# Attention in a two-layer block: scores of the two components in one paired group or one after the other with a turn between

## The chip, the cores and the metric

The kernel runs on one core of a Trainium2 chip. The metric is the device time of one execution in microseconds; lower is better. A whole block of two layers is one launch. The change touches one stage of it, the attention of the first layer.

## What is computed

The reference adds 16 meta tokens to 1024 tokens of width 1024 and runs two layers. The first mixes by a state space model (S5) and, beside it, by differential attention; the second by a gated recurrence; behind each mixer stand a projection, a norm, a router and a mixture of experts. All of it is in float32. The attention has 4 heads; a head has two components of 64 dimensions each for queries and keys, and one set of values of 128 dimensions:

```python
def block(args):
    q_blk, c_blk = args
    s = jnp.einsum('bqhcd,bkhcd->bchqk', q_blk, k) * scale
    mask = cid[None, :] <= c_blk[:, None]
    p = jax.nn.softmax(jnp.where(mask, s, NEG_INF), axis=-1)
    w = p[:, 0] - lam * p[:, 1]
    return jnp.einsum('bhqk,bkhe->bqhe', w, v)
```

Two softmaxes are taken over the same keys, one for each component, and their difference with a learned factor weighs the values. The mask lets a query see its own chunk of 64 tokens and all chunks before it.

## The kernel before

The stages run one behind the other, with a barrier between them. `attention` (line 633) is cut into 36 units, a unit being a head and a tile of queries. Tile 0 has the 16 meta tokens, tiles 1 to 8 have 128 queries each. A unit with tile `qi` needs the first n = 16 + 128 qi keys, so n runs through 16, 144, 272, ..., 1040. Heads 0 to 2 take their tiles in rising order, head 3 in falling order (line 660).

For a unit u the work passes over three engines:

- TensorE, `scores(u)` (line 700): for each component c a matmul of the queries (64 rows of the array: rows 0 to 63 for c = 0, rows 64 to 127 for c = 1) with up to 512 keys at a time, into the PSUM area `S[(2u + c) % 3]` of 1024 columns. There are three such areas. A second, short matmul of `hide` and `ones` (48 or 64 columns, for n = 528 another of 16) adds the mask to the last chunk. For n = 1040 the last 16 keys go into a small area of their own, `tail`. The matmuls of the two components are written in turns: one of c = 0, one of c = 1, for the same part of the keys, the last part first. A float32 matmul has two records in the trace, a transpose has one.
- VectorE, `minimum(u, c)` (line 851): the row minimum of a component's scores (scores are kept with their sign turned by the scale -1 of the exponential).
- ScalarE, `exps(u, c)` (line 799): the exponential of the scores from PSUM into `prob`, with the row sums. Its end (`exp_done`) gives the area of PSUM free.
- VectorE, `combine(u)` (line 870): the two components into one tile of weights `w`.
- TensorE, `turn(u, j)` (line 729): transposes of up to four blocks of `w` into the one PSUM area `tp`; ScalarE and VectorE in turns copy it away (`copies`, line 775). A unit with more than four blocks has two or three such groups j.
- TensorE, `weigh(u, j)` (line 742): turned weights times values, into `po`; ScalarE's `out` (line 812) takes the result away, VectorE's `square` (line 886) sums its squares.

Each engine runs its own list in order, and semaphores tie them together. On TensorE the list (lines 757 to 764) is: scores of unit u + 1, then by groups the turn of unit u - 1 and the products of unit u - 2. `scores(u)` waits once, for `exp_done` of 2u - 1: the exponential of component 0 of the unit ahead, which frees the area of its own component 1.

```python
for u in range(-1, U + LAG):
    if u + 1 < U:
        scores(u + 1)
    for j in range(max(groups)):
        if 0 <= u - LAG + 1 < U and j < groups[u - LAG + 1]:
            turn(u - LAG + 1, j)
        if 0 <= u - LAG < U and j < groups[u - LAG]:
            weigh(u - LAG, j)
```

Of the kernel before, what the change touches and what calls it, by code (L numbers as in the profile page):

```python
# [632 lines left out]
def attention(nc, K, A):  # L633
# [12 lines left out]
    hide, ones = at("hide", [P]), at("ones64", [64])  # L646
# [13 lines left out]
    units = [(hd, qi) for hd in range(HEADS - 1) for qi in range(NT)] + [(HEADS - 1, qi) for qi in reversed(range(NT))]  # L660
    U = len(units)
    groups = [-(-(qi + 1) // PER) for _, qi in units]
    first_group = [sum(groups[:u]) for u in range(U + 1)]
    tails = [sum(qi == NT - 1 for _, qi in units[:u]) for u in range(U + 1)]
    with ExitStack() as ctx:
        S = [ctx.enter_context(nc.psum_tensor(f"scores{i}", [P, WIDE], F32)) for i in range(3)]
# [5 lines left out]
        @block.sync  # L672
        def _(sp):
            with nc.allow_non_contiguous_dma(reason="small parameters"):
                for i, n in enumerate(("lq1", "lk1", "lq2", "lk2")):
                    sp.dma_start(lq[i][:], A["l0_da_" + n].rearrange("(a d) -> a d", a=1).to_broadcast([P, HEAD_DIM])).then_inc(loaded, 16)
                sp.dma_start(g[:], A["l0_da_subln_g"].rearrange("(p a) -> p a", a=1)).then_inc(loaded, 16)
            load_w_out(sp, K, 0)
# [11 lines left out]
        def cuts(u):  # L690
            q0, m = TILES[units[u][1]]
            n = q0 + m
            ends = list(range(0, n, 512)) + [n]
            return q0, m, n, list(zip(ends, ends[1:]))

        @block.tensor
        def _(pe):
            pe.wait_ge(hide_made, 4)

            def scores(u):  # L700

                hd, qi = units[u]
                q0, m, n, parts = cuts(u)
                if u:
                    pe.wait_ge(exp_done, 2 * u - 1)
                if n > WIDE and u > LAG + 1:
                    pe.wait_ge(o_copied, u - LAG - 1)
                rows = [slice(64 * c, 64 * c + 64) for c in range(2)]
                if n > WIDE:
                    for c in range(2):  # L710
                        pe.matmul(tail[0:m, c, :], K.qT[rows[c], hd, q0:q0 + m], K.kT[rows[c], hd, WIDE:n], start=True, stop=False)
                        pe.matmul(tail[0:m, c, :], hide[rows[c], 0:m], ones[rows[c], 0:n - WIDE], start=False, stop=True).then_inc(tail_made, 1)
                        pe.wait_ge(tail_made, 2 * tails[u] + c + 1)
                for a, b in reversed(parts):
                    if a >= WIDE:
                        continue
                    place = lambda c, a, b: S[(2 * u + c) % 3][0:m, a:b]
                    lo = max(a, n - 64) if qi else b
                    for c in range(2):
                        last = pe.matmul(place(c, a, b), K.qT[rows[c], hd, q0:q0 + m], K.kT[rows[c], hd, a:b], start=True, stop=lo >= b)  # L720
                        if lo >= b and a == 0:
                            last.then_inc(s_ready, 1)
                    if lo < b:
                        for c in range(2):
                            last = pe.matmul(place(c, lo, b), hide[rows[c], 0:m], ones[rows[c], 0:b - lo], start=False, stop=True)
                            if a == 0:
                                last.then_inc(s_ready, 1)

            def turn(u, j):
                hd, qi = units[u]  # L730
                q0, m = TILES[qi]
                n = first_group[u] + j
                if j == 0:
                    pe.wait_ge(w_ready, u + 1)
                if n:
                    pe.wait_ge((turned_a, turned_v)[(n - 1) % 2], (n - 1) // 2 + 1)
                for kt in range(PER * j, min(PER * j + PER, qi + 1)):
                    k0, kk = TILES[kt]
                    last = pe.transpose(tp[0:kk, kt % PER, 0:m], w[u % 2][0:m, k0:k0 + kk], K.ident[0:m, 0:m])
                last.then_inc(turned, 1)  # L740

            def weigh(u, j):
                hd, qi = units[u]
                m = TILES[qi][1]
                n = first_group[u] + j
                pe.wait_ge((turned_a, turned_v)[n % 2], n // 2 + 1)
                if j == 0 and u:
                    pe.wait_ge(o_copied, u)
                if j == 0 and tails[min(u + LAG + 2, U)]:
                    pe.wait_ge(tail_done, tails[min(u + LAG + 2, U)])  # L750
                for kt in range(PER * j, min(PER * j + PER, qi + 1)):
                    kk = TILES[kt][1]
                    last = pe.matmul(po[0:m, :], wT[u % 2][0:kk, kt, 0:m], K.v_rows[0:kk, kt, P * hd:P * hd + P], start=kt == 0, stop=kt == qi)
                if j == groups[u] - 1:
                    last.then_inc(o_ready, 1)

            for u in range(-1, U + LAG):
                if u + 1 < U:
                    scores(u + 1)
                for j in range(max(groups)):  # L760
                    if 0 <= u - LAG + 1 < U and j < groups[u - LAG + 1]:
                        turn(u - LAG + 1, j)
                    if 0 <= u - LAG < U and j < groups[u - LAG]:
                        weigh(u - LAG, j)

            for i in range(NT):
                q0, m = TILES[i]
                pe.wait_ge(on_ready, i + 1)
                if i >= 2:
                    pe.wait_ge(oT_copied, i - 1)  # L770
                for h in range(HEADS):
                    last = pe.transpose(S[i % 2][:, P * h:P * h + m], o_sb[0:m, i, P * h:P * h + P], K.ident[0:m, 0:m])
                last.then_inc(oT_ready, 1)
# [1576 lines left out]
```

## Time and profile before

| what | value |
|---|---|
| median of 3 runs | 2592.74 us (2589.94 to 2603.44) |
| the profiled execution's own time | 2592.88 us |
| its span | 2591.1 us |
| mean granted clock of TensorE over the span | 0.937 |
| TensorE busy over the span | 2293.0 us, 88% |
| attention, from its first matmul to its last product | 352 to 557 us |

A granted clock of 1 is 2.4 GHz, one of 0.5 is 1.2 GHz. In the trace's views "idle before" stands in brackets behind a row, with the operation that ended the idle time; x4 is a count of records merged into one row, whose time runs from the first start to the last end. A form such as 64*128 64x512 is an array tile of 64 rows and 128 columns, through which 512 columns stream. Ends of matmuls are modelled; the distance between starts tells how long the array streamed.

### The profile page before, as it was taken

How to read it: one execution, taken by the hardware profiler on the slowest of the kernel's cores; microseconds unless marked ns; L12 is line 12 of the kernel's file. 1: busy time of each engine (PE TensorE's matmuls, PEld its weight loads, DVE VectorE, ACT ScalarE, POOL GpSimd, SP SyncE). 2: the span in 40 equal slices, each digit the busy share in tenths (PEclk: the TensorE clock that was granted, in tenths of full speed). 3: DMA queues.
4: the chain of work that ended last, by engine and by line, in shares of the span. 5: the costliest groups of instructions: out<-in, count | busy, mean ns of one | idle time of the engine just before them, and what ended most of it. 6: DMA issues, size and time to landing. Idle time of an engine off the chain costs nothing. (4 is left out here: it accounts for less than half of the span.)

```text
span 2591.1 us, 33356 instructions
## 1 busy us (share of the span) xinstructions
PE 2293.0 (88%) x13399; PEld 1284.7 (50%) x13399; DVE 819.2 (32%) x1629; ACT 488.7 (19%) x894; POOL 307.9 (12%) x265
## 2 busy tenths in 40 slices
PE   6999977889958999999968999999976999999984
PEld 4788535554545445445524555554444445545441
DVE  5652135543251111111107455554333101111115
ACT  2222123331101000000003444441110000000001
POOL 5252000001101101110002000001100111111102
PEclk9999988899968999999988999999977999999997
DMA  4100010011239998998948211111209998999965
GB/s 144 35 33 1 17 67 1 1 29 42 73 139 390 421 405 346 410 409 363 412 188 260 66 35 28 29 38 47 65 17 385 420 412 340 411 410 369 412 270 211
DMA packets 141990, 528.01 MB, mean 204 GB/s; under 512 B 38098, under 2 KB 61170, under 8 KB 125456
## 3 DMA queue, kind: packets, MB, share of 16 engines
q1 hardware_dynamic: 115632, 465.57, 45.9%
q0 software_dynamic: 13600, 40.52, 4.1%
q10 hardware_dynamic: 12608, 19.82, 2.3%
q8 instruction: 107, 1.75, 0.3%
q14 instruction: 43, 0.35, 0.0%
HBM read 492.04 MB, written 40.50 MB: 206 GB/s over the span
## 5 line engine op out<-in xcount | busy, mean ns | idle before, releaser
L1698 PE MATMUL l_main_pgu<-l_w_ring,l_ex_xT 128*64 128x256 f32 (+1 forms) x4992 | 489.2, 385 | 15.7 <-DMA l_w_ring<-in_l_moe_w_gate 13.5
L1698 PEld LDWEIGHTS l_main_pgu<-l_w_ring,l_ex_xT 128*64 128x64 f32 (+1 forms) x4992 | 294.2, 130 | 200.8 <-issue 40.7
L1744 PE MATMUL l_main_py<-l_w_ring,l_ex_hT 128*64 128x512 f32 (+1 forms) x1248 | 239.3, 595 | 1.6 <-DVE l_ex_hT L1803 1.6
L1695 PE MATMUL l_main_pgu<-l_w_ring,l_ex_xT 128*128 128x512 f32 x384 | 177.6, 618 | 20.8 <-DMA l_w_ring<-in_l_moe_w_gate 20.8
L1803 DVE COPY l_ex_hT<-l_main_ph 128x256 f32<-128x256 f32 (+1 forms) x78 | 36.3, 466 | 419.8 <-PE l_main_ph L1719 419.8
L1799 DVE TENSOR_TENSOR l_ex_hid<-l_ex_sil,l_main_pgu 128x256 f32<-128x256 f32 (+1 forms) x78 | 36.1, 462 | 351.6 <-PE l_main_pgu L1698 270.2
L2130 PE MATMUL lru_pr<-h2T,lru_wz 128*128 128x352 f32 (+1 forms) x480 | 143.2, 459 | 3.8 <-ACTq L2179 3.8
L1744 PEld LDWEIGHTS l_main_py<-l_w_ring,l_ex_hT 128*64 128x64 f32 (+1 forms) x1248 | 71.5, 128 | 136.6 <-issue 129.6
L2135 PE MATMUL lru_pg<-h2T,lru_wz 128*128 128x512 f32 x320 | 139.0, 592 | 0.0
L1695 PEld LDWEIGHTS l_main_pgu<-l_w_ring,l_ex_xT 128*128 128x128 f32 x384 | 74.2, 198 | 113.4 <-issue 88.0
L1780 ACT ACTIVATE l_ex_sil<-l_main_pgu 128x256 f32<-128x256 f32 (+1 forms) x78 | 32.5, 417 | 486.3 <-PE l_main_pgu L1698 336.6
L1643 POOL DMA_INDIRECT expert_rows<-l_ex_yb,half_row x66 | 66.1, 1002 | 444.0 <-issue 219.6
L2130 PEld LDWEIGHTS lru_pr<-h2T,lru_wz 128*128 128x128 f32 x480 | 91.6, 192 | 53.8 <-ACTq L2179 4.2
L2009 PE MATMUL l_cps<-l_y,ident 128*128 128x512 f32 (+1 forms) x136 | 68.5, 659 | 53.3 <-DMA l_y<-expert_rows 53.3
L283 PE MATMUL s_pa<-hT,w_in 128*128 128x260 f32 x512 | 114.7, 383 | 0.0
L985 POOL TENSOR_TENSOR H<-H,l_ln_bias 128x1024 f32<-128x1024 f32 (+1 forms) x30 | 70.6, 2353 | 352.4 <-DVE H L973 352.4
L1050 PE MATMUL lru_pr<-w_out,y1T 128*128 128x512 f32 x240 | 106.5, 601 | 0.0
L283 PEld LDWEIGHTS s_pa<-hT,w_in 128*128 128x128 f32 x512 | 96.9, 190 | 16.4 <-issue 1.7
L2135 PEld LDWEIGHTS lru_pg<-h2T,lru_wz 128*128 128x128 f32 x320 | 60.8, 190 | 73.6 <-issue 71.8
L1630 POOL DMA_INDIRECT l_ex_xb<-h_rows,x_idx x38 | 37.4, 984 | 412.6 <-PE l_main_px L1667 262.5
L1766 ACT COPY l_ex_xT<-l_main_px 128x512 f32<-128x512 f32 (+1 forms) x52 | 27.5, 529 | 285.4 <-PE l_main_px L1667 285.4
L720 PE MATMUL scores<-kT,qT 64*128 64x512 f32 (+5 forms) x224 | 59.6, 615 | 17.6 <-ACT prob L807 14.7
(420 smaller groups left out, 2821.1 us busy)
## 6 DMA issues: line engine op xcount, KB each, us to landing
l_w_ring<-in_l_moe_w_gate SPq DMA_DIRECT2D x64, 2048.0 KB, 19.1
l_w_ring<-in_l_moe_w_up SPq DMA_DIRECT2D x64, 2048.0 KB, 23.5
l_w_ring<-in_l_moe_w_down SPq DMA_DIRECT2D x64, 2048.0 KB, 21.2
l_y<-expert_rows ACTq DMA_DIRECT2D x32, 512.0 KB, 6.5
h_rows<-H SPq DMA_DIRECT2D x24, 512.0 KB, 5.2
lru_wz<-in_l_w_in SPq DMA_DIRECT2D x20, 512.0 KB
w_in<-in_l_w_in SPq DMA_DIRECT2D x3, 2048.0 KB, 8.4
w_out<-in_l_w_out SPq DMA_DIRECT2D x2, 2560.0 KB, 12.6
```

The costliest lines, as they stand in the source:

```text
L283: last = pe.matmul(pa[n % 2][:, 0:STEPS], w[:, k, P * (f % HEADS):P * (f % HEADS) + P], hT[:, k, j, :], start=k == 0, stop=k == KD - 1)
L720: last = pe.matmul(place(c, a, b), K.qT[rows[c], hd, q0:q0 + m], K.kT[rows[c], hd, a:b], start=True, stop=lo >= b)
L985: pool.tensor_tensor(z, z, self.bias[0:m, :], ALU.add).then_inc(self.h_ready, 1)
L1050: last = pe.matmul(po[j % 2][h][0:m, :], self.slices[k][:, t0:t0 + m], self.w_out[:, k, 512 * h:512 * h + 512], start=k == 0, stop=k == ns ...
L1630: pool.indirect_dma_start(xb[xn % 2][0:m, :], None, K.h1_dram, bass.IndirectOffsetOnAxis(ap=index, axis=0)).then_inc(gathered[xn % 2], 16)
L1643: pool.indirect_dma_start(y_halves, bass.IndirectOffsetOnAxis(ap=K.half_row[:, it.column:it.column + 1], axis=0), yb[i % 2][:, 0:512], Non ...
L1695: last = pe.matmul(out[:], x[:, k, :], w[0][:, k, :], start=k == 0, stop=k == KD - 1)
L1698: last = pe.matmul(out[HALF * h + o:HALF * h + o + m, 0:256], x[:, k, it.at + o:it.at + o + m], w[n][:, k, 256 * h:256 * h + 256], start=k ...
L1744: last = pe.matmul(py[b][HALF * h + o:HALF * h + o + m, :], hT[:, c % 2, HALF * (c // 2) + o:HALF * (c // 2) + o + m], ws[n][:, c, 512 * h ...
L2009: last = pe.matmul(ps[i % 2][h][0:m, :], K.ident[0:m, 0:m], y[j % YB][0:m, 512 * h:512 * h + 512], start=k == 0, stop=k == 1)
L2130: last = pe.matmul(pr[j][:, 0:c], wz[par][:, k, 0, :], K.hT[:, k, o:o + c], start=k == 0, stop=k == KD - 1)
L2135: last = pe.matmul(pgt[j][:, 0:c], wz[par][:, k, 1, :], K.hT[:, k, N_META + o:N_META + o + c], start=k == 0, stop=k == KD - 1)
```

## The change

On TensorE alone, `scores(u)` becomes three pieces. `score_tail(u)` holds the matmuls for the last 16 keys of the largest tile, with their wait. `scores(u, c)` holds all parts of one component, the first keys first, and waits for `exp_done` of x - 2 with x = 2u + c, which is what frees area x % 3. For c = 1 this is the wait of before; for c = 0 it is one exponential earlier. The semaphore `s_ready` still counts one for each component, in the same order. In the list of the engine, component 0 of unit u + 1 comes first, then the first turn of unit u - 1, then component 1 of unit u + 1, then the first products of unit u - 2. The other engines' code is the same.

```diff
--- before.py
+++ after.py
@@ -697,12 +697,10 @@
         def _(pe):
             pe.wait_ge(hide_made, 4)
 
-            def scores(u):
+            def score_tail(u):
 
                 hd, qi = units[u]
                 q0, m, n, parts = cuts(u)
-                if u:
-                    pe.wait_ge(exp_done, 2 * u - 1)
                 if n > WIDE and u > LAG + 1:
                     pe.wait_ge(o_copied, u - LAG - 1)
                 rows = [slice(64 * c, 64 * c + 64) for c in range(2)]
@@ -711,20 +709,23 @@
                         pe.matmul(tail[0:m, c, :], K.qT[rows[c], hd, q0:q0 + m], K.kT[rows[c], hd, WIDE:n], start=True, stop=False)
                         pe.matmul(tail[0:m, c, :], hide[rows[c], 0:m], ones[rows[c], 0:n - WIDE], start=False, stop=True).then_inc(tail_made, 1)
                         pe.wait_ge(tail_made, 2 * tails[u] + c + 1)
-                for a, b in reversed(parts):
+
+            def scores(u, c):
+
+                hd, qi = units[u]
+                q0, m, n, parts = cuts(u)
+                x, rows = 2 * u + c, slice(64 * c, 64 * c + 64)
+                if x >= 3:
+                    pe.wait_ge(exp_done, x - 2)
+                area = S[x % 3]
+                for a, b in parts:
                     if a >= WIDE:
                         continue
-                    place = lambda c, a, b: S[(2 * u + c) % 3][0:m, a:b]
                     lo = max(a, n - 64) if qi else b
-                    for c in range(2):
-                        last = pe.matmul(place(c, a, b), K.qT[rows[c], hd, q0:q0 + m], K.kT[rows[c], hd, a:b], start=True, stop=lo >= b)
-                        if lo >= b and a == 0:
-                            last.then_inc(s_ready, 1)
+                    last = pe.matmul(area[0:m, a:b], K.qT[rows, hd, q0:q0 + m], K.kT[rows, hd, a:b], start=True, stop=lo >= b)
                     if lo < b:
-                        for c in range(2):
-                            last = pe.matmul(place(c, lo, b), hide[rows[c], 0:m], ones[rows[c], 0:b - lo], start=False, stop=True)
-                            if a == 0:
-                                last.then_inc(s_ready, 1)
+                        last = pe.matmul(area[0:m, lo:b], hide[rows, 0:m], ones[rows, 0:b - lo], start=False, stop=True)
+                last.then_inc(s_ready, 1)
 
             def turn(u, j):
                 hd, qi = units[u]
@@ -756,10 +757,13 @@
 
             for u in range(-1, U + LAG):
                 if u + 1 < U:
-                    scores(u + 1)
+                    score_tail(u + 1)
+                    scores(u + 1, 0)
                 for j in range(max(groups)):
                     if 0 <= u - LAG + 1 < U and j < groups[u - LAG + 1]:
                         turn(u - LAG + 1, j)
+                    if j == 0 and u + 1 < U:
+                        scores(u + 1, 1)
                     if 0 <= u - LAG < U and j < groups[u - LAG]:
                         weigh(u - LAG, j)
```

What moves on TensorE, at a large tile: first head, n = 912 (scores in parts of 512 and 400), with the turn of the tile of 656 keys and the products of the one of 528. Before:

```order
L720 MATMUL scores<-kT,qT 128x400 x2
L725 MATMUL scores<-ones_2689,hide 128x64 x2
L720 MATMUL scores<-kT,qT 128x512 x2
L739 MATMUL turned_w<-ident,w_rows_2678 16x128
L739 MATMUL turned_w<-ident,w_rows_2678 128x128 x3
L753 MATMUL weighed<-v_rows,w_cols_2679 128x128 x4
L739 MATMUL turned_w<-ident,w_rows_2678 128x128 x2
L753 MATMUL weighed<-v_rows,w_cols_2679 128x128
```

With the change:

```order
L725 MATMUL scores<-kT,qT 128x512
L725 MATMUL scores<-kT,qT 128x400
L727 MATMUL scores<-ones_2689,hide 128x64
L740 MATMUL turned_w<-ident,w_rows_2678 16x128
L740 MATMUL turned_w<-ident,w_rows_2678 128x128 x3
L725 MATMUL scores<-kT,qT 128x512
L725 MATMUL scores<-kT,qT 128x400
L727 MATMUL scores<-ones_2689,hide 128x64
L754 MATMUL weighed<-v_rows,w_cols_2679 128x128 x4
L740 MATMUL turned_w<-ident,w_rows_2678 128x128 x2
L754 MATMUL weighed<-v_rows,w_cols_2679 128x128
```

The rows with x2 were one matmul of each component next to each other. Now all of component 0 stands ahead of the turn (`turned_w`) and all of component 1 behind it, ahead of the first products (`weighed`).

At a small tile, second head, n = 272, where the turn in front is that of the 16 meta tokens and the products are those of the largest tile (nine blocks in three groups). Before:

```order
L720 MATMUL scores<-kT,qT 128x272 x2
L725 MATMUL scores<-ones_2689,hide 128x64 x2
L739 MATMUL turned_w<-ident,w_rows_2678 16x16
L753 MATMUL weighed<-v_rows,w_cols_2679 128x128 x9
```

With the change:

```order
L725 MATMUL scores<-kT,qT 128x272
L727 MATMUL scores<-ones_2689,hide 128x64
L740 MATMUL turned_w<-ident,w_rows_2678 16x16
L725 MATMUL scores<-kT,qT 128x272
L727 MATMUL scores<-ones_2689,hide 128x64
L754 MATMUL weighed<-v_rows,w_cols_2679 128x128 x9
```

The second component's two matmuls moved behind the turn; nothing else did.

## Rows read from the trace of the kernel before

**Rows 1.** The page, busy us (share of the span) and instructions of an engine.
```profile
PE 2293.0 (88%) x13399; PEld 1284.7 (50%) x13399; DVE 819.2 (32%) x1629; ACT 488.7 (19%) x894; POOL 307.9 (12%) x265
```

**Rows 2.** Busy time by stretch, attention: length, busy us and instructions, clock, DMA.
```profile
352.00:558.00 206.00, 157.89 (x940) 108.37 (x940) 112.91 (x327) 84.03 (x249) 0.14 (x1) 0.83 0.06 22
```

**Rows 3.** Waits in 352 to 558 us: who waited for whom, us, times, longest.
```profile
ACT prob L807 <- DVE row_min L859: 52.6, 52, 3.2
...
PE scores L720 <- ACT prob L807: 14.7, 11, 8.9
...
PE turned_w L739 <- ACT w_cols L792: 11.7, 10, 2.1
PE turned_w L739 <- DVE w_cols L792: 10.9, 6, 3.6
```

**Rows 4.** TensorE in time, one tile of head 1: start, us, what [idle before].
```profile
418.36 0.52 PE L720 MATMUL scores<-kT,qT 64*128 64x144 f32 x4 [0.42 <-ACT prob L807]
...
418.87 1.08 PE L720 MATMUL scores<-kT,qT 64*128 64x512 f32 x4
419.88 0.60 PE L739 MATMUL turned_w<-ident,w_rows 128*16 128x128 f32 x4
...
421.87 0.73 PE L720 MATMUL scores<-kT,qT 64*128 64x272 f32 x4 [0.33 <-ACT prob L807]
```

**Rows 5.** TensorE in time, the projection behind attention.
```profile
568.74 3.59 PE L1050 MATMUL l_po<-w_out,yT 128*16 128x512 f32 x8 [1.57 <-PEq L2275]
572.17 3.60 PE L1050 MATMUL l_po<-w_out,daT 128*16 128x512 f32 x8
```

**Rows 6.** TensorE's busy time by stretch, cut at starts of units.
```profile
361.40:374.60 13.20, 10.77 (x54) 0.54 0.59 216
374.60:382.80 8.20, 7.02 (x47) 1.00 0.00 0
382.80:400.70 17.90, 13.79 (x68) 0.81 0.01 1
400.70:421.90 21.20, 18.50 (x146) 1.00 0.00 1
421.90:451.90 30.00, 20.57 (x92) 0.72 0.00 1
451.90:480.00 28.10, 25.31 (x169) 0.88 0.00 1
480.00:528.30 48.30, 35.94 (x188) 0.81 0.00 1
528.30:553.00 24.70, 23.30 (x170) 0.95 0.01 2
```

**Rows 7.** The nine stretches at half clock, first and last, and their sum.
```profile
352.00:373.00 21.00, 9.51 (x50) 0.53 0.57 207
...
526.50:529.90 3.40, 3.40 (x23) 0.60 0.02 5
sum 72.20, PE 51.58; mean PE 5.73
```

**Rows 8.** TensorE in time, large tiles of head 1.
```profile
427.54 0.33 PE L739 MATMUL turned_w<-ident,w_rows 128*128 128x128 f32 x1 [2.05 <-DVE w_cols L792]
427.80 1.37 PE L720 MATMUL scores<-kT,qT 64*128 64x400 f32 x4
...
429.28 2.03 PE L720 MATMUL scores<-kT,qT 64*128 64x512 f32 x4
...
435.56 0.69 PE L739 MATMUL turned_w<-ident,w_rows 128*128 128x128 f32 x2 [2.28 <-DVE w_cols L792]
...
440.22 2.08 PE L720 MATMUL scores<-kT,qT 64*128 64x512 f32 x4
```

**Rows 9.** The projection: its stretch, and a group of its records with its shape.
```profile
568.70:582.50 13.80, 13.76 (x32) 1.00 0.63 132
...
L1050 PE MATMUL l_po<-w_out,yT 128*16 128x512 f32 x16 | 7.2, 592 | 1.6 <-PEq L2275 1.6
```

## Prediction

> **What bounds the kernel now.** I read the page first. TensorE is busy for 88% of the whole span [rows 1], but this change touches one stage, so that share says nothing about it. The busy time by stretch comes next. Attention lies at 352 to 558 us, 206 us in which the array is busy for 157.9, VectorE for 112.9, ScalarE for 84.0, at a mean granted clock of 0.83 [rows 2]. No engine is full: the stage is a ring of waits. The view of waits names them [rows 3]: ScalarE's exponentials wait for VectorE's minima (52.6 us), the scores for the exponentials (14.7, of which 8.9 is the single wait in the opening, for small parameters), and the turns for the copies that ScalarE and VectorE make of the turn ahead (11.7 and 10.9). The order of the array's work in time shows where: between small tiles it waits 0.4 us or nothing, between large ones 2 us and more [rows 4, 8].
>
> The same view shows what the two components do. At full clock four records of 64x512 (two matmuls, one of each component, in two passes each) begin at 418.87 and the next work begins at 419.88: 1.0 us for four [rows 4]. One record of 512 columns alone takes 0.43 (eight from 568.74 to 572.17, all begun within 3.43 us [rows 5]), so four in a row would take 1.7. The two components, one in the upper 64 rows of the array and one in the lower, now stream side by side.
>
> The last thing to see is the clock. It is 1.2 GHz (granted 0.5) in an opening stretch, 352 to 373, and in eight later ones; all nine are 72.2 us with 51.58 of busy array, so the eight are 51.2 us with 42.1 of busy array [rows 7]. Ahead of them stand waits: 2.05 us ahead of 427.54, where a pair of 512 then takes 2.03 us rather than 1.1, and 2.28 ahead of 435.56 [rows 8].
>
> **Part 1, the pair is taken apart: cost.** No matmul is added; the count of passes is the same. But a component's passes now stream alone. With 0.43 us for 512 columns and two passes for a matmul, a component of n columns adds 4n/2400 us of array time at full clock, and its masking matmul (48 to 64 columns) some 0.11. Over 36 units n adds up to 18,944 (at most 1024 counts, since the tail's 16 columns were never paired): 31.6 us, and 3.4 for 32 masks, 35 in all, twice that at half clock. Idle array time takes part of it up. By stretches cut at starts of units [rows 6], idle is the length less the busy time:
> 361.4 to 374.6, n = 144 to 528, at half clock: adds 5.3, idle 2.4, leaves 2.9.
> 374.6 to 382.8, n = 656 and 784: adds 2.6, idle 1.2, leaves 1.4.
> 382.8 to 400.7, n = 912 and 1040: adds 3.4, idle 4.1, leaves 0.
> 400.7 to 421.9, n = 16 to 656: adds 3.9, idle 2.7, leaves 1.2.
> 421.9 to 451.9, n = 784 to 1040: adds 4.9, idle 9.4, leaves 0.
> 451.9 to 480.0, n = 16 to 784: adds 5.3, idle 2.8, leaves 2.5.
> 480.0 to 528.3, five large units: adds 8.3, idle 12.4, leaves 0.
> 528.3 to 553.0, n = 656 to 144: adds 3.9, idle 1.4, leaves 2.5.
> That is **10.5 us** later. If none could be hidden it would be 35 and more; if all, 0.
>
> **Part 2, the turn between the components.** The array goes from scores to turn to scores to products: two more changes a unit between matmuls that use 64 rows and ones that use all. The trace has the price of one: the lone turn at 427.54 has 128 columns, 0.11 us of streaming, and the scores behind it begin at 427.80, so 0.15 goes for the change [rows 8]. The other kind, from scores to full height, is bounded by 0 and the same 0.15; I take 0.05, since the turn at 419.88 begins as soon as two pair steps of about 0.5 have streamed [rows 4]. 0.2 in each of the 24 units of the stretches that have no idle left is **4.8 us**; in the large units it is covered.
> The Trainium skill speaks against this placing: "TensorEngine Tiling (Array Packing)", section Key Properties, says that a change of tiling mode, and not just of tile, drains the array. An estimate by it: the drain is what a record lasts (0.59 us by the mean of its group [rows 9]) beyond the 0.43 to the next start, 0.16, twice a unit, 24 times: 7.7 us in place of 4.8, and the forecast would be 3 us later.
> By queue: the second component's scores now stand behind the turn, which waits until its weights are combined and the previous turn is copied away. VectorE takes the minimum of the second component only after the first one's and after the combining of the tile ahead (lines 895 to 901), so a turn of 0.6 us in front of those scores [rows 4] should delay nobody while the array runs at full clock. I cost it at nothing; where that cover is thin, it shows as a wait for the second component's scores. No DMA and no other queue is touched.
>
> **Part 3, the head start.** The first component now waits only for its own area, one exponential earlier than before, and is ready when its own passes are (0.43 a step, where a pair takes 0.5 [rows 4, 5]). In the 12 units with n of 784 and more VectorE gets it about 0.2 us sooner for that: **-2 us**. Bounds: 0, and the 5.8 us of waits for exponentials that stand outside the opening [rows 3].
>
> **Part 4, the clock: the term that decides.** The waits that stand ahead of the slow stretches are the idle time which the added passes fill: 1.3 to 1.7 us of them a unit at n = 784 to 1040, against waits of 2.05 and 2.28 [rows 8]. If the later slow stretches go, 42.1 us of busy array at half clock becomes 21: up to **-21 us**. The lower end is 0, or worse, as a rival. The opening stretch follows the wait for parameters and stays. Whether a pass that fills half the array keeps the clock up is not shown in this stage, where it never runs alone for long. The nearest row is the projection behind the stage: 32 records of 128*16, an eighth of the array's columns, fill 568.7 to 582.5 and the clock stays 1.00 [rows 5, 9]. A partly filled array counted as active there, so I take it that it does here.
> The Trainium skill, "TensorE: Matmul & The Clock Gate", Part 1, has the throttled state as the default and activity as what lifts it; it does not say how half the rows count.
>
> **Sum.** 10.5 + 4.8 - 2 - 21 = -7.7; the profiled execution took 2592.88 us (1.8 outside its span) and the median of the three shown is 2592.74, so they stand together. 2592.9 - 7.7 = 2585.2; I round the head start up a little, since its bound is far, and forecast **2584.5 us**. A measurement of this kernel can tell about 0.5%, 13 us, from no change.
>
> **Rivals.**
> A, the clock does not follow, slower. If a pass of 64 rows alone counts for half of what a full one does, a unit's activity is what it was, the stretches stay, and the time runs longer with the added passes in them. Then 10.5 + 4.8 - 2, and 3 more for the units in slow stretches, where the addition (3.4 us for n = 1024) outgrows the idle time of some: +16, **2609 us**. For it: nothing in the stage shows a lone half-height pass; against: rows 5 and 9. The point from which it decides: if less than 13 of the 21 us come back, the kernel is slower than before. Partly so (half the stretches go) is +3, 2596. Chance of this rival 0.2.
> B, the large units shorten too, faster. There the ring of minimum, exponential, copy and turn sets the pace, and the first component may start one exponential earlier. If each of the 12 units with n of 784 and more gains 0.6 us beyond the forecast, it is -7 more: **2577 us**. For it: minima and copies are the largest waits of the stage [rows 3]; against: the turn behind the first component still waits on what it waited on. Chance 0.2.
> C, the passes were never free side by side: if the pair shares one stream, a lone pass of 512 takes 0.25 and not 0.43, nothing is added, and it is -23, **2570 us**. Against: a pair's 1.0 us is just over two lone full-height steps (0.86), which is what two streams of their own give; for a shared one, half-height passes would have to stream at twice the rate of rows 5. Chance 0.03.
>
> **How the numbers follow.** Forecast 0.57, A 0.2, B 0.2, C 0.03. The forecast's own range is -16 to +3 (the clock's term between two thirds and all, the covered part up or down by 5). 8 in 10 are held by 2573 to 2608: from just below B to A. Faster by over 0.5% (below 2579.8): C, over half of B and a quarter of the forecast, 0.28. Slower by over 0.5% (above 2605.7): most of A, 0.14. The same: 0.58.
>
> **What would show it.** In the changed profile: the scores' records of the two components apart, each record of 512 columns 0.43 after the last; array busy in the stage some 15 us above 157.9 even with a higher clock; mean granted clock of the stage 0.92 or more, with only the opening low; small units longer (n = 656: 3.5 us from 418.36 to 421.87 now, 4.3 then), large ones shorter (the 12.4 us of n = 912 from 427.80 to 440.22 becomes 9 or less) [rows 4, 8]. If the clock's mean stays at 0.83, Part 4 is wrong; if small units keep their length, Part 1 is.

## The result, and the profile after

| | before | with the change |
|---|---|---|
| median | 2591.94 us (4 runs) | 2646.28 us (2642.2 to 2665.33, 4 runs) |
| ratio, 95% interval | | 1.0206 [1.0165, 1.0247] |
| profiled span | 2591.1 us | 2646.8 us |
| attention: first score matmul to first projection matmul | 216.5 us | 263.9 us |
| the same stretch, time at 1.2 GHz | 78.5 us | 160.4 us |
| span behind it | 2022.4 us | 2030.1 us |

The kernel is some 54 us slower. The stage that the change touches is 47.4 us longer in the profiled executions. The 8 us behind it are in stages whose code is the same; in the twelve experiments below that part lies between 2016 and 2027 us, so the 2030 of this execution is just above all of them. I put it down to the difference between executions; no run shows its cause.

The page's row for TensorE, against [rows 1]:

```profile
PE 2378.4 (90%) x13399; PEld 1340.9 (51%) x13399; DVE 821.2 (31%) x1629; ACT 489.5 (18%) x894; POOL 307.8 (12%) x265
```

The stage by stretch (length, busy us and instructions of TensorE, weight loads, VectorE, ScalarE, GpSimd, then clock and DMA), to be read beside [rows 2]:

```profile
352.00:616.00 264.00, 243.87 (x976) 166.93 (x976) 121.59 (x338) 91.42 (x259) 0.57 (x4) 0.70 0.05 17
```

VectorE and ScalarE did nearly what they did before (118.8 and 90.1 us over the same instructions in the kernel before, 352 to 568.7), while TensorE is busy for 243.9 us of 264: it is now the bound. Its mean granted clock in the stage is 0.70.

The stage cut where the granted clock changes, TensorE alone; this answers to [rows 6, 7] (left out are 489.6 to 496.4, with a slow stretch of 3.4 us from 493, and what follows 602.2, with one of 10.2):

```profile
353.00:421.30 68.30, 59.48 (x162) 0.51 0.18 64
421.30:438.40 17.10, 17.10 (x111) 0.97 0.00 0
438.40:489.60 51.20, 49.72 (x132) 0.51 0.00 1
496.40:530.50 34.10, 33.10 (x178) 0.99 0.00 1
530.50:557.80 27.30, 26.73 (x72) 0.52 0.00 1
557.80:602.20 44.40, 43.08 (x256) 0.99 0.00 1
```

In the slow stretches the array is all but full: 49.72 us of 51.2 in the one from 438.4. Before the change, slow stretches followed waits and lasted 3.4 to 10.2 us, with the opening one of 20.5 the longest. Now one lasts 51 us with next to no wait in it, and the opening one 68, with one long wait, the 8.2 us for small parameters.

At three of the four rises of the clock (421.3, 489.6, 557.8) TensorE had just run turns and products of the full height one after the other, with no scores between them. Ahead of 489.6:

```profile
485.59 2.37 PE L754 MATMUL weighed<-v_rows,w_cols 16*128 16x128 f32 x8
488.02 0.90 PE L740 MATMUL turned_w<-ident,w_rows 128*128 128x128 f32 x3
488.72 1.06 PE L754 MATMUL weighed<-v_rows,w_cols 128*128 128x128 f32 x4
```

(The first row carries the form of its first record; the products behind it use 128 rows.) Where it falls at 438.4, there is no wait in the 17.1 us ahead; the last 4.1 of them hold scores of 64 rows, two transposes and one product of 16 rows.

TensorE in time, at a large tile at half clock (395.54 on, n = 912) and at a small one at full clock (434.27 on, n = 400), against [rows 4, 8]:

```profile
395.54 3.41 PE L725 MATMUL scores<-kT,qT 64*128 64x512 f32 x4
398.75 0.53 PE L727 MATMUL scores<-ones,hide 64*128 64x64 f32 x2
399.20 1.02 PE L740 MATMUL turned_w<-ident,w_rows 128*16 128x128 f32 x4
400.15 3.41 PE L725 MATMUL scores<-kT,qT 64*128 64x512 f32 x4
...
434.27 0.94 PE L725 MATMUL scores<-kT,qT 64*128 64x400 f32 x2
435.05 0.33 PE L727 MATMUL scores<-ones,hide 64*128 64x64 f32 x2
435.31 0.39 PE L740 MATMUL turned_w<-ident,w_rows 128*16 128x128 f32 x2
```

At full clock component 0 of n = 400 takes from 434.27 to 435.31, 1.04 us, and so does component 1 behind the turn. The pair of the kernel before took 1.04 us for both (412.40 to 413.44): doubled, as expected. At half clock component 0 of n = 912 takes 3.66 us. A row of scores here, x4 or x2, belongs to one component; before, it held both.

The waits, against [rows 3]:

```profile
ACT prob L811 <- DVE row_min L863: 79.5, 51, 4.7
DVE row_min L863 <- PE scores L727: 68.7, 42, 4.3
...
PE scores L725 <- ACT prob L811: 8.2, 1, 8.2
```

The exponentials wait for the minima, and the minima for the scores (68.7 us): the others wait for the array. The array's own wait for exponentials outside the opening is gone.

### The profile page after: what moved, and what is told of

It reads as the page before. It is cut to its first block and busy times, and to the rows that moved or that the text cites. A ratio compares the mean times of both kernels' runs of the same rounds, so it can differ in the third digit from the quotient of the medians.

```text
span 2646.8 us, 33356 instructions
## 1 busy us (share of the span) xinstructions
PE 2378.4 (90%) x13399; PEld 1340.9 (51%) x13399; DVE 821.2 (31%) x1629; ACT 489.5 (18%) x894; POOL 307.8 (12%) x265
## 5 line engine op out<-in xcount | busy, mean ns | idle before, releaser
L725 PE MATMUL scores<-kT,qT 64*128 64x512 f32 (+4 forms) x224 | 119.6, 658 | 11.1 <-ACT prob L811 8.2
## 6 DMA issues: line engine op xcount, KB each, us to landing
l_w_ring<-in_l_moe_w_gate SPq DMA_DIRECT2D x64, 2048.0 KB, 23.3
```

The lines of the kernel that those rows point to most:

```text
L725: last = pe.matmul(area[0:m, a:b], K.qT[rows, hd, q0:q0 + m], K.kT[rows, hd, a:b], start=True, stop=lo >= b)
```

## The experiments

The theories. **T1**: passes that use 64 of the array's 128 rows, one component alone, do not lift a clock that has fallen as passes of the full height do (the expectations say that one counts "for about half"; no run measures that share). **T2**: the order (turn between, early start) makes the waits. **T3**: only the doubled streaming counts, the clock is incidental. Ratios are to the kernel before on the same chip in the same batch. Its median was 2594.35 for the first four runs below, 2596.86 for the next three and for the one with full height in the large tiles alone, 2597.39 for the two that change one half of the tiles, 2595.42 for the two with idle work.

### Full-height passes in the changed order

```diff
+qz = [[at(f"q_tall{b}{c}", [P]) for c in range(2)] for b in range(2)]
...
+for u in range(U):
...
+    for c in range(2):
+        r64 = slice(64 * c, 64 * c + 64)
+        pool.tensor_copy(qz[u % 2][c][r64, 0:m], K.qT[r64, hd, q0:q0 + m]).then_inc(qz_ready, 1)
...
-last = pe.matmul(area[0:m, a:b], K.qT[rows, hd, q0:q0 + m], K.kT[rows, hd, a:b], ...)
+last = pe.matmul(area[0:m, a:b], qz[u % 2][c][:, 0:m], K.kT[:, hd, a:b], ...)
```

> The changed kernel with its order, its waits and its count and length of passes, but each score matmul of one component now uses all 128 rows of the array: GpSimd copies the component's 64 rows of queries into a tile whose other 64 rows are zero (the mask is added twice over, which masks the same). Theory T1 (a pass of 64 rows alone counts for about half of what keeps the clock up): the mean granted clock of attention rises from 0.69 to 0.9 or more, the stage (first score matmul to first projection matmul) falls from 264 us to about 200, the kernel to 2580 to 2592 us. Theory T2 (the order and its waits keep the array idle or slow, whatever its height): clock and time stay, 2640 to 2650 us. T3 (only the doubled streaming at an unchanged clock): the same as T2, no change.

Measured: 2579.69 us median, ratio 0.9939 [0.9918, 0.9961]. The stage took 207.6 us, of which 44.4 at half clock. Its busy times and clock, and its two longest waits for minima:

```profile
352.00:560.30 208.30, 181.52 (x977) 134.18 (x978) 119.90 (x336) 89.39 (x259) 27.00 (x76) 0.89 0.06 22
```

```profile
ACT prob L826 <- DVE row_min L878: 46.2, 51, 2.1
ACT prob L828 <- DVE row_min L886: 31.3, 7, 8.0
```

The number and the columns of the passes are those of the changed kernel; the weights of half of the rows are zeros, while both components' keys stream past. The clock is 0.89 instead of 0.70 and the stage 56 us shorter. T3 falls, and so does T2 in the form that it has here, as a cost of the order whatever the height; T1 stands. It is also 0.6% faster than the kernel before, at the lower edge of what T1 forecast.

The edit takes away one more thing: the changes between matmuls of 64 rows and of 128. In the tile of n = 656 at full clock they cost 0.48 us (Part 2 under "Why the prediction was wrong"), which over 36 units is some 17 us, an estimate from one tile. So of the 56 us some 39 are left for the clock. No run separates the two within the stage.

### Full-height passes in the old order

```diff
-last = pe.matmul(place(c, a, b), K.qT[rows[c], hd, q0:q0 + m], K.kT[rows[c], hd, a:b], ...)
+last = pe.matmul(place(c, a, b), qz[u % 2][c][:, 0:m], K.kT[:, hd, a:b], ...)
```

> The kernel before with its order and its one wait, but the score matmuls use all 128 rows as in the first run, so the two components can no longer stream side by side. T1: the clock of the stage is 0.9 or more, the time 2585 to 2600: the doubled streaming is paid back by the clock. T3: the doubled streaming costs its price at the clock of before, 2600 to 2620. Beside the first run it shows what the order alone is worth with streaming equal: within 6 us by T1, the changed order some 30 slower by T2.

Measured: 2612.79 us, ratio 1.0063 [1.0038, 1.0087]; stage 230.9 us, 54.6 of them slow. Beside the run above:

```profile
352.00:583.80 231.80, 191.01 (x976) 135.16 (x976) 119.64 (x336) 89.46 (x259) 20.40 (x75) 0.88 0.05 19
```

```profile
ACT prob L822 <- DVE row_min L874: 65.0, 52, 3.5
ACT prob L824 <- DVE row_min L882: 38.5, 7, 10.5
```

The clock is high, as T1 has it, but the time is above T1's 2585 to 2600. I had expected both orders within 6 us and they are 33 apart, in the other direction than T2's: with equal streaming the **changed order is the better one**. Of the 33 us, 23.3 lie in the stage of the profiled executions (230.9 against 207.6) and 7.5 behind it, where the code is the same. With the matmuls of the components in turns, component 0 is complete only when nearly all of component 1 is too. In the changed order its minimum can run beside component 1's passes: the two rows of waits for minima are 77.5 us there and 103.5 in the old order (46.2 + 31.3 against 65.0 + 38.5). Two other differences between the orders, the turn's place and the head start, are taken away one at a time further down.

### The clock and the shape of a pass, by itself

```diff
+pe.wait_ge(rested, 2)
+run(36, 64, 128)     # matmuls, rows, columns of weights; 512 columns stream
+run(20, 128, 128)
+run(36, 64, 128)
+run(20, 128, 128)
+run(36, 32, 128)
+run(20, 128, 128)
+run(36, 128, 64)
+run(20, 128, 128).then_inc(rest, 1)
+pe.wait_ge(rested, 4)
+run(36, 64, 128, both=True)
...
+pe.wait_ge(rested, 6)
+run(36, 128, 64)
```

This phase stands between attention and projection and computes nothing that is used.

> The kernel before with one more phase behind attention that only measures (some 350 us longer): dense streams of float32 matmuls with 512 columns of one shape each, on an array that has just rested for 9 us or has just run at full height. T1: from rest, lone 64-row passes stay at 1.2 GHz (0.86 us a pass) for their whole stream, while full-height passes behind them lift the clock; 64-row passes in pairs from rest lift it as full ones do; 32-row passes let it fall from full speed. Rival T1b (what counts is busy time, not height): every dense stream lifts the clock within its first 10 us, whatever its height. For 64 columns of 128: no forecast by either, it tells whether width counts too.

Measured, TensorE in stretches inside the bursts, in this order: 64 rows from rest; full; 64 rows behind full; 32 rows behind full; 64 columns behind full; pairs of 64 rows from rest (two rows); 64 columns from rest (two rows). Between the rows shown the bursts of full height ran at 1.00 too.

```profile
581.00:642.00 61.00, 61.00 (x72) 0.50 0.00 0
645.00:659.00 14.00, 14.00 (x34) 1.00 0.00 0
663.00:690.00 27.00, 27.00 (x65) 1.00 0.00 1
714.00:769.00 55.00, 55.00 (x65) 0.50 0.00 0
790.00:815.00 25.00, 25.00 (x59) 1.00 0.00 0
845.00:849.00 4.00, 3.80 (x10) 0.50 0.00 0
850.00:875.00 25.00, 25.00 (x118) 1.00 0.00 1
897.50:900.50 3.00, 3.00 (x4) 0.50 0.00 0
901.00:920.00 19.00, 19.00 (x46) 1.00 0.00 0
```

- From rest, **64-row passes alone stay at half clock for all 61 us of a full stream** (72 passes, 0.85 us each). Full-height passes behind them have 1.00 from 645 on, 3 us after they began.
- Behind full-height passes the same 64-row stream keeps 1.00 for 27 us. So in these bursts half height holds a clock that is up and does not lift one that is down.
- Behind full-height passes 32 rows let it fall, to 0.50 for 55 us.
- Pairs of 64 rows from rest, which began at 845.2, have 1.00 from 849.9 on.
- 64 of 128 columns keep it (25 us) and, from rest, have 1.00 from 901.1 on, 3.7 us after they began. **Half the height alone did not lift the clock; half the width did.**

Each of these shapes ran once or twice, in this order alone.

T1b falls. The stage shows the same: a stage whose scores are half-height passes gets a fallen clock back late. What let it fall at 438.4, behind 17.1 us without a wait, the bursts do not tell, since there 64-row passes held it; that stays open. The Trainium skill, "TensorE: Matmul & The Clock Gate", Part 1, says that the throttled state is the default and that activity releases it; the 61 us of dense 64-row passes at 1.2 GHz do not agree, if every dense stream is taken for activity.

### Only the turn's place undone

```diff
 scores(u + 1, 0)
+scores(u + 1, 1)
 for j in range(max(groups)):
     ...
-    if j == 0 and u + 1 < U:
-        scores(u + 1, 1)
```

> The changed kernel with component 1 written right behind component 0 and the turn behind both, so that only the turn's place is undone. T1: the passes still stream alone for the most part, the clock stays near 0.7, the time falls by 2 to 10 us, to 2636 to 2644. T2 (the turn in between is what costs, by its wait and by the two more changes of height): at least 30 us come back, below 2616.

Measured: 2604.33 us, ratio 1.0042 [1.0020, 1.0065], stage 240.7 us. I was wrong and T2's number held: 42 us come back. But not by T2's mechanism. In time, at n = 272 and at the start of n = 528:

```profile
424.39 0.73 PE L725 MATMUL scores<-kT,qT 64*128 64x272 f32 x4
424.95 0.34 PE L727 MATMUL scores<-ones,hide 64*128 64x64 f32 x4
425.22 0.18 PE L740 MATMUL turned_w<-ident,w_rows 16*16 16x16 f32 x1
...
429.54 1.12 PE L725 MATMUL scores<-kT,qT 64*128 64x512 f32 x2
430.50 0.31 PE L727 MATMUL scores<-ones,hide 64*128 64x48 f32 x2
430.65 0.70 PE L725 MATMUL scores<-kT,qT 64*128 64x16 f32 x3
```

At n = 272 the program has four records of component 0 and then four of component 1, yet four of 64x272 lie within 0.73 us, which is what a pair took before (421.87 in [rows 4]): the records of component 1 began 13 ns behind those of component 0. **The array took the matmul of the other half ahead of ones that stood before it in the list.** At n = 528 component 0 has four matmuls, eight records. Its two records of 512 stream alone for 1.12 us, and the first of component 1 begins only beside the last ones (the three records from 430.65, two of 16 columns and one of 512). With the turn between, none overlap: in the change's trace component 1 begins behind the turn each time. So the turn's place cost because it kept the halves apart, which the next run bears out. The profiled execution is a late one, 2615.71 us, with 157.0 us of its stage at 1.2 GHz; over its whole span the mean clock was 0.919, as in the change. Eight of the ten executions, 2598 to 2612 us, had 0.927 to 0.931, against 0.931 to 0.936 for the kernel before: where the components overlap, most of the clock came back as well. How the 42 us divide between the shorter passes and the clock is not shown.

### The same with full height

The edit is that of the run above on the first experiment.

> The first run (full height everywhere, order of the change) with component 1 right behind component 0 and the turn behind both. At full height the components cannot overlap, so if the 42 us that the second run gave back came from overlap of the two halves of the array, the turn's place is worth little here: within 4 us of 2579.7. If the turn's place costs by its wait or by the change of height as such, 10 us or more faster.

Measured: 2582.81 us, ratio 0.9948 [0.9926, 0.9970], the same as the first experiment's within the intervals. Where nothing can overlap, the turn's place is worth nothing that can be measured.

### The head start, at full and at half height

```diff
-if x >= 3:
-    pe.wait_ge(exp_done, x - 2)
+if u:
+    pe.wait_ge(exp_done, 2 * u - 1)
```

At full height the condition stays `x >= 3`; only the count waited for changes.

> The first run with the wait of the kernel before: component 0 too waits for the exponential that frees component 1's area. It prices the head start by itself at a high clock: my estimate from the waits for exponentials of the kernel before is 2 to 6 us slower than 2579.7. If the whole 33 us by which the first run beats the third came from the head start, it is 2600 or more; if they came from component 0 being complete before component 1 is written, nearly nothing.

Measured: 2581.29 us, ratio 0.9940 [0.9922, 0.9958], against 0.9939 with the head start. It is worth nothing that can be measured, and neither is the turn's place, so what sets the two orders at full height apart is that component 0 is complete before component 1 begins. (The order of a component's own parts, last or first keys first, changed with it and was not tried alone.)

> The changed kernel with its 64-row passes, and only the head start undone. T1: the array at half clock is the bound, so a later start costs little: 2642 to 2655 us. If the head start itself did harm (T2, component 0 issued early blocks the array's list at the turn), it is 2630 or less.

Measured: 2660.73 us (2645.49 to 2662.95), ratio 1.0232 [1.0191, 1.0273] against 1.0206 [1.0165, 1.0247] of the change. It is above T1's 2642 to 2655 and far from T2's 2630: the head start did no harm. Whether it helped with 64-row passes these intervals don't tell; the profiled stage is 286.1 us, with 201.4 at 1.2 GHz, against 263.9 and 160.4.

### One half of the tiles at a time

The scores are written as in the change (64 rows, alone) or as before (pairs, ahead of the turn), by size of tile.

```diff
+mode = lambda n: "lone" if n > 656 else "pair"     # the other run: "pair" if n > 656 else "lone"
```

> 64-row passes of one component alone, in the order of the change, for the 12 tiles with n of 784 and more; pairs as before for the 24 smaller ones. T1: the clock falls in the large tiles and is lifted again by the pairs in the small ones, so about the large tiles' half of the loss is left: 2600 to 2625 us. If the loss sat in the small tiles alone (no idle time to hide in), it is 2590 or less.

> The other half: pairs for the large tiles, 64-row passes alone for the small ones. T1: once the opening or a wait has let the clock fall, half-height passes in the small tiles do not lift it, so the stage stays slow there too: 2605 to 2635 us. If only the doubled streaming counted, the 10.5 us of my sum: about 2603.

Measured: 2608.92 us, ratio 1.0048 [1.0018, 1.0078], with the 12 large tiles changed; 2630.23 us, 1.0125 [1.0091, 1.0159], with the 24 small ones. The stage of the first, then of the second:

```profile
352.00:584.40 232.40, 204.02 (x976) 139.97 (x976) 120.16 (x337) 90.80 (x259) 0.98 (x7) 0.75 0.05 19
```

```profile
352.00:608.80 256.80, 218.83 (x976) 153.47 (x972) 120.05 (x336) 89.88 (x259) 0.49 (x4) 0.70 0.05 18
```

12 and 33 us, together 44 or 45 of the 54. Three quarters of it sit in the small tiles, where I had found 10.5 us: they have hardly any idle time, and with half-height passes they no longer repair the clock (153.8 us slow against 78.5 before; 115.9 in the other run).

### Full height in the large tiles, pairs in the small

```diff
+mode = lambda n: "tall" if n > 656 else "pair"
```

> Full-height passes in the order of the change for the 12 tiles with n of 784 and more (order tall, as in the first run), and the pairs of the kernel before, as one group ahead of the turn, for the 24 smaller ones. If the first run gained in the large tiles through the clock and the earlier first minimum and paid with doubled streaming in the small ones, whose array had next to no idle time, this is faster than it: 2565 to 2577 us against 2579.7. If the doubled streaming in the small tiles is what held the clock up, it is 2580 or more.

Measured: 2585.89 us, ratio 0.9950 [0.9931, 0.9970]. No faster than full height everywhere, whose interval it overlaps; the saving of 3 to 15 us that I expected isn't there, and the time is where the expectation's other case had it, 2580 or more. The stage has 58.0 us at half clock against 44.4, with 174.0 us of busy array against 181.5.

### The clock alone, with the pairs kept

```diff
+def fill(count):
+    for _ in range(count):
+        pe.matmul(out_bank[:, P + 2 * N_META:512], K.ident[:], K.kT[:, 0, 0:352], start=True, stop=True)
...
+if u == 0:
+    fill(12)
...
+if j == 0 and u + LAG + 1 < U and cuts(u + LAG + 1)[2] > 656:
+    fill(2)
```

> The kernel before, its pairs and order untouched, with idle work for the array alone: 12 full-height matmuls of 352 columns (0.59 us each at full speed) into unused PSUM columns during the wait for parameters in the opening, and 2 of them ahead of the first products beside each tile with n of 784 and more, where the array goes on to wait 1.1 to 3.6 us. It prices the clock by itself. T1 (activity by height and time; the clock of these waits is the whole of my term of 21 us): the slow stretches in the large tiles and the end of the one in the opening go, the stage's clock is 0.92 or more, 2570 to 2585 us on a base of 2592. If the clock rises and the time stays within 5 us, the term was over-sized, since the large tiles then wait for VectorE and ScalarE instead.

Measured: 2589.04 us, ratio 0.9977 [0.9965, 0.9989]; stage 210.9 us:

```profile
352.00:563.20 211.20, 180.24 (x1049) 122.04 (x1050) 119.00 (x337) 90.14 (x259) 0.22 (x3) 0.88 0.06 21
```

The clock is below the 0.92 and the time above the 2570 to 2585 that T1 had. Slow time fell from 78.5 to 51.2 us (five slow stretches stayed behind 381) and the stage by 5.6 us: 0.2 us for each us of slow clock that went, where my term had 0.4 (21 for 51.2). The two fills ahead of a large tile's products take 1.3 us of array time themselves, so this rate is that of the run and may be low for the clock alone. With pairs the large tiles go on to wait for VectorE behind them: 2.64 us at 447.96.

> The first run (full height, order of the change, 0.9939 of the kernel before) with 12 full-height idle matmuls in the opening wait. The array works at half clock for some 6 us behind that wait in the first run; if they run at full speed, 3 us come back: ratio about 0.993. No change beyond the interval if they are behind VectorE anyway.

The edit is the `fill(12)` of the last run on the first experiment. Measured: 2584.30 us, ratio 0.9955 [0.9939, 0.9970] against 0.9939 [0.9918, 0.9961]: no gain, though the opening's slow stretch went from 13.6 to 5.5 us.

## Why the prediction was wrong

The time lies 38 us above the range and on the other side of the forecast. By its own steps:

- **Part 1** (35 us of streaming, 10.5 of them showing at the clock of before): the streaming was right where the clock was up. A unit of n = 656 takes 4.52 us at full clock in the changed kernel, 4.3 were forecast, 3.5 before:

```profile
512.25 1.37 PE L725 MATMUL scores<-kT,qT 64*128 64x512 f32 x4
...
514.25 1.37 PE L725 MATMUL scores<-kT,qT 64*128 64x512 f32 x4
...
516.77 1.58 PE L725 MATMUL scores<-kT,qT 64*128 64x512 f32 x4
```

  The 10.5 were not measured alone. The nearest run is the one of full height in the old order, where the halves cannot overlap either: its stage is 14.4 us longer than before, with less slow time (54.6 us against 78.5).
- **Part 2** (4.8): at full height the same unit takes 4.04 us:

```profile
415.23 1.27 PE L740 MATMUL scores<-kT,q_tall 128*128 128x512 f32 x4
...
416.94 1.27 PE L740 MATMUL scores<-kT,q_tall 128*128 128x512 f32 x4
...
419.27 1.48 PE L740 MATMUL scores<-kT,q_tall 128*128 128x512 f32 x4
```

  So the four changes of height in it cost 0.48. By the starts of records, a change to 64 rows costs 0.19 (0.09 ahead of its first pass, 0.10 in that pass), one from scores to the turn 0.09, one from scores to the products nothing. The two more that I counted, into and out of the turn, are 0.28 by this, where I had 0.20. The queue's part, which I costed at nothing, is nothing at full height. At half height the turn's place is worth 42 us, but as the price of Part 1, the halves kept apart, and of the clock that went with it.
- **Part 3** (-2): the early start is worth nothing that can be measured. That component 0 is complete before component 1 begins is worth some 23 us of the stage at full height, in place of 2. The sign was right and the size far off; with 64-row passes it was not measured.
- **Part 4 is the step that failed**: "A partly filled array counted as active there, so I take it that it does here." The row it rested on was partly filled in width, 16 of 128 columns. In the bursts 64 of 128 columns lifted a fallen clock and 64 of 128 rows, alone, did not in 61 us. So in place of -21 us for a clock that rises came one that stayed down for 160.4 us of the stage instead of 78.5. Full height in the same order took 56 us off the stage, some 39 of them for the clock by the estimate above.
- **Its price** may have been off too: with the pairs kept, 27 us less of slow clock came with 5.6 us, so the 51.2 would be worth some 10 and not 21 (an estimate at that rate, with the fills' own time in it).
- **Rival A** had the mechanism and the wrong size, +16. It kept the nine stretches as they were. It missed that half-height passes do not lift the clock in the small, dense tiles either: n = 656 then takes 8.4 us (377.2 to 385.6) rather than 4.5. The chance of 0.2 was too low for a mechanism against which stood a row of another kind only.
- **Rival C**'s sum left out the 4.8 of Part 2: -2 and -21 with it make -18, 2575 us, and not 2570.

Whether the forecast would have held with the clock up is not shown. The first experiment is 14.7 us faster than the kernel before in the same batch, 8.9 of them in the stage, but it also has no changes to and from 64 rows.

## What to carry to other kernels

Two matmuls of 64 rows in different halves of the array took one matmul's time here (1.04 us at n = 400); taken apart they took twice the time and no longer lifted the clock, so ask of every split what it does to the granted clock. If operands allow it, filling the idle rows' weights with zeros kept the clock up (0.89 against 0.70), at the price of the overlap. When a row is to stand for one that the trace lacks, it must be alike in the very property in question: a row with few columns says nothing on few rows.

## What the runs showed of the hardware that I had not expected

- Height made the difference to the clock, width did not: 64 rows alone stayed at 1.2 GHz for 61 us of dense streaming from rest, and at 2.4 GHz for 27 us behind full-height passes; with 32 rows the clock fell; with 64 columns from rest it rose after 3.7 us.
- Rows whose weights are zero did as well as full ones: the first experiment's extra rows are such, and its stage has 0.89.
- TensorE started a matmul of the other half of the array ahead of records written before it: 13 ns behind the first of four at n = 272, and beside the last ones of eight at n = 528.
- At full clock a change from full-height to 64-row matmuls cost 0.19 us, one from 64 rows to a turn 0.09 (n = 656).
